# Neighbourhood attention: the second head's probabilities scaled by GpSimd, the bias loads issued between its steps

## What is computed

```python
s_loc = einsum(qr, kr) * scale + bias          # 8 rows x 32 columns of keys around the query
s_loc = where(mask, s_loc, -inf)
s_ctx = einsum(qr, kc) * scale                 # the 256 context keys
p = softmax(concatenate([s_loc, s_ctx], -1), -1)
o = einsum(p_loc, vr) + einsum(p_ctx, vc)
y_c = o * silu(cz)
```

## Time and profile before

| | |
|---|---|
| runs, median (lowest to highest) | 3112.86 us (3111.77 to 3113.13) |
| the profiled execution, its own time | 3115.25 us |
| its span, first to last instruction | 3113.5 us |
| TensorE busy | 2975.4 us, 96% of the span |
| DVE busy | 1497.5 us, 48% |
| ScalarE busy | 1155.9 us, 37% |
| GpSimd busy | 147.6 us, 5% |

### The profile page before, as it was taken

One profiled execution on the slowest core, in us unless ns is written; L12 is line 12 of the kernel. 1 busy time (PEld: TensorE's weight loads), 2 busy tenths in 40 slices (PEclk: granted clock), 3 DMA queues, 4 the chain that ended last, 5 costly groups with the idle time before them and its releaser, 6 DMA issues.

```text
span 3113.5 us, 38501 instructions
## 1 busy us (share of the span) xinstructions
PE 2975.4 (96%) x15486; PEld 2424.6 (78%) x15486; DVE 1497.5 (48%) x2136; ACT 1155.9 (37%) x1828; POOL 147.6 (5%) x206
## 2 busy tenths in 40 slices
PE   7999999999999998989999999999999899999998
PEld 5767888777788887867888878868877678888776
DVE  4645454645454657267252542263444735353454
ACT  4335233425352344136233331163221634251352
POOL 1000000010000000000000400100000000120100
PEclk9999999999999999999999999999999999999999
DMA  4232322331332221110211211211111022222322
GB/s 178 95 142 101 122 108 101 113 122 68 109 107 91 97 90 54 68 48 4 74 42 62 90 67 54 95 59 61 54 61 68 21 77 67 90 88 81 112 75 81
DMA packets 44460, 256.79 MB, mean 82 GB/s; under 512 B 6344, under 2 KB 6352, under 8 KB 20512
## 3 DMA queue, kind: packets, MB, share of 16 engines
q1 hardware_dynamic: 30528, 204.30, 18.5%
q0 software_dynamic: 13792, 50.51, 5.0%
HBM read 250.51 MB, written 4.28 MB: 82 GB/s over the span
## 4 chain that ended last, share of the span: by engine, by line
PE 84%; DVE 9%; ACT 3%; issue 1%; DMA 1%; POOL 1%; DVEq 0%; SPq 0%; ACTq 0%
PE PS L805 13%; PE PS L806 13%; PE PS L807 13%; PE PS L786 7%; PE PS L785 7%; PE PS L787 7%; PE PS L751 2%; PE PS L750 2%; PE PS L749 2%; DVE SMALL L2392 2%; PE PS L986 1%; DMA W<-in_w 1%; PE PS L698 1%; PE PS L594 1%; PE PS L596 1%
## 5 line engine op out<-in xcount | busy, mean ns | idle before, releaser
L805 PE MATMUL PS<-HHX,WHX 128*128 128x512 f32 (+1 forms) x1456 | 511.2, 351 | 9.9 <-DVE WLX L2242 7.0
L806 PE MATMUL PS<-HL,WHX 128*128 128x512 f32 (+1 forms) x1456 | 512.3, 352 | 0.0
L1559 ACT ACTIVATE WHX<-W 128x2048 fp32r<-128x2048 f32 (+1 forms) x102 | 174.6, 1712 | 578.9 <-DMA W<-in_w 391.3
L807 PE MATMUL PS<-HHX,WLX 128*128 128x512 f32 (+1 forms) x1024 | 357.6, 349 | 0.0
L2242 DVE TENSOR_TENSOR WLX<-W,WHX 128x2048 fp32r<-128x2048 f32 x60 | 137.5, 2292 | 383.4 <-ACT WHX L1559 383.4
L805 PEld LDWEIGHTS PS<-HHX,WHX 128*128 128x128 f32 x1456 | 278.8, 191 | 48.4 <-DVE WLX L2242 7.8
L806 PEld LDWEIGHTS PS<-HL,WHX 128*128 128x128 f32 x1456 | 277.5, 191 | 36.6
L786 PE MATMUL PS<-HL,WH 128*128 128x512 f32 x672 | 265.4, 395 | 0.0
L785 PE MATMUL PS<-HH,WH 128*128 128x512 f32 x672 | 263.3, 392 | 0.0
L2242 DVE TENSOR_TENSOR WL<-W,WH 128x2048 fp32r<-128x2048 f32 x68 | 155.9, 2292 | 221.7 <-ACT WH L1559 221.6
L787 PE MATMUL PS<-HH,WL 128*128 128x512 f32 x672 | 261.7, 389 | 0.0
(11 more groups left out here) (533 smaller groups left out, 5902.4 us busy)
## 6 DMA issues: line engine op xcount, KB each, us to landing
W<-in_w SPq DMA_DIRECT2D x172, 1024.0 KB, 4.7
XC<-in_wm POOLq DMA_DIRECT2D x12, 1024.0 KB, 5.1
H<-in_wm POOLq DMA_DIRECT2D x12, 1024.0 KB, 5.7
W<-in_wb SPq DMA_DIRECT2D x24, 512.0 KB, 3.2
W<-in_w SPq DMA_DIRECT2D x8, 768.0 KB, 4.1
ARENA<-mrow POOLq DMA_DIRECT2D x12, 256.0 KB, 4.1
ARENA<-wrow POOLq DMA_DIRECT2D x12, 256.0 KB, 4.6
PR<-in_nbias POOLq DMA_DIRECT2D x12, 256.0 KB, 2.9
```

The costliest lines, as they stand in the source:

```text
L805: pe.matmul(dst, wh[:, s, c], hi[:, k, t0:t1], start=k == 0, stop=False)
L806: pe.matmul(dst, wh[:, s, c], lo[:, k, t0:t1], start=False, stop=False)
L807: mm = pe.matmul(dst, wl[:, s, c], hi[:, k, t0:t1], start=False, stop=k == kb - 1)
L1559: act.activation(dst[:, s, 0:n], W[:, s, 0:n], ACT.Copy).then_inc(wh_ready[s], 1)
```

## The change

- DVE scales head 0 alone; GpSimd scales head 1, with `tensor_scalar` by the same reciprocal, and counts a new semaphore `na_far`. TensorE's transposes of head 1 wait for `na_far`.
- The reciprocal counts a new semaphore `na_rec` in place of DVE's own step counter; DVE waits for it as it did for its own, and GpSimd waits for it ahead of its scaling.
- GpSimd goes through the steps in order. It issues load `i` after the scaling of the last step that uses load `i - 2`, and no longer waits for `na_max`.
- Two semaphores are saved elsewhere: the eight loads of the LRU weights count `loaded_pool`, so that whoever waits for the start's loads waits for nine of GpSimd's, and `ml_w` becomes a second count of `ml_l`.

```diff
-        eng.wait_ge(loaded_pool, 16)
+        eng.wait_ge(loaded_pool, 16 * 9)
...
-        pe.wait_ge(sem("lru_w"), 16 * 8)
+        pe.wait_ge(loaded_pool, 16 * 9)
...
-                pe.wait_ge(sem("na_probs"), past("na_probs", ly) + 2 * e["s"] + hh + 1)
+                done = ("na_probs", "na_far")[hh]
+                pe.wait_ge(sem(done), past(done, ly) + e["s"] + 1)
...
-                    act.activation(WQ[0:8, :, :], WQ[0:8, :, :], ACT.Exp).then_inc(sem("ml_w"), 1)
+                    act.activation(WQ[0:8, :, :], WQ[0:8, :, :], ACT.Exp).then_inc(sem("ml_l"), 1)
...
-            own.link(dve.reciprocal(SMALL[:, 32 + p:32 + p + n], SMALL[:, 16 + p:16 + p + n]))
+            dve.reciprocal(SMALL[:, 32 + p:32 + p + n], SMALL[:, 16 + p:16 + p + n]).then_inc(sem("na_rec"), 1)
+            dve.wait_ge(sem("na_rec"), past("na_rec", ly) + e["s"] + 1)
             v = NE[:, e["s"] % 2, :, :].rearrange("p a b -> p (a b)")
-            for i in range(n):
+            for i in range(n // 2):
                 c = slice(i * w, (i + 1) * w)
                 ins = dve.tensor_scalar(v[:, c], v[:, c], SMALL[:, 32 + p + i:33 + p + i], None, ALU.mult)
-                if (i + 1) * w % T == 0:
-                    ins.then_inc(sem("na_probs"), 1)
+            ins.then_inc(sem("na_probs"), 1)
...
-                pool.wait_ge(sem("ml_w"), past("ml_w", st.layer) + 1)
+                pool.wait_ge(sem("ml_l"), past("ml_l", st.layer) + 2)
...
-                for i in range(2, 12):
-
-                    last = max(e["s"] for e in steps if e["load"] == i - 2 and not e["ctx"])
-                    pool.wait_ge(sem("na_max"), past("na_max", ly) + last + 1)
-                    bias(ly, i)
+                for e in steps:
+                    p = 4 * (e["s"] % 2)
+                    pool.wait_ge(sem("na_rec"), past("na_rec", ly) + e["s"] + 1)
+                    v = NE[:, e["s"] % 2, 1, :]
+                    k = 2 if e["ctx"] else 1
+                    for i in range(k):
+                        c = slice(i * T // k, (i + 1) * T // k)
+                        ins = pool.tensor_scalar(v[:, c], v[:, c], SMALL[:, 32 + p + k + i:33 + p + k + i], None, ALU.mult)
+                    ins.then_inc(sem("na_far"), 1)
+                    for i in range(2, 12):
+                        if max(x["s"] for x in steps if x["load"] == i - 2 and not x["ctx"]) == e["s"]:
+                            bias(ly, i)
```

More of the change, by code:

```diff
@@ L467, in build @@
         ml_zm=n_ml, ml_o=n_ml, ml_dens=n_mu, ml_divf=n_mu, ml_divb=n_mu, ml_rs=n_mu, ml_scaled=n_mu,
-        ml_turned=n_mu, ml_y=n_mu, ml_w=1, ml_stored=64, ml_rows=1, ml_l=1, ml_ac=1, ml_emc=1,
+        ml_turned=n_mu, ml_y=n_mu, ml_stored=64, ml_rows=1, ml_l=2, ml_ac=1, ml_emc=1,
         bz_silu=6, cv_done=4, gate_mm=2, gate_f=2, gate_cols=2, wg_hi=1, wg_lo=1, wg_loaded=16, bqk=8, cv_scaled=8, rope_loaded=32,
-        rope_done=8, na_probs=2 * n_na, na_max=n_na, na_values=n_na, v_stored=16 * 8, v_blocks=16 * 7,
+        rope_done=8, na_probs=n_na, na_rec=n_na, na_far=n_na, na_max=n_na, na_values=n_na, v_stored=16 * 8, v_blocks=16 * 7,
         **{f"ml_bm{k}": 16 * slot_uses[k] for k in range(4)}, **{f"ml_bw{k}": 16 * state_uses[k] for k in range(4)})
@@ L2878, in _ @@
                                         64 * half:64 * half + 64],
-                                   lru_w[g, half, :, 2 * q:2 * q + 2, :]).then_inc(sem("lru_w"), 16)
+                                   lru_w[g, half, :, 2 * q:2 * q + 2, :]).then_inc(loaded_pool, 16)
         pool.wait_ge(w_ready[1], 16)
```

## The result

The changed kernel takes 3147.73 us, median of 4 runs (3144.22 to 3152.13), against 3112.99 us for the kernel before, measured beside it: ratio 1.0106, 95% interval 1.0094 to 1.0118. It is slower, as forecast, but by 1.1% where 0.5% was forecast; it lies 7 us above the range. The profiled execution took 3149.49 us, 34.2 more than the one of before.

The account below looks back on a forecast made before the run. TensorE was taken to bound the kernel, with DVE close behind. Less DVE work (-2.6), head 1 late (+3.6) and late bias loads (+14.4) summed to +15.4 us: 3128.3 us against the runs' median, range 3119 to 3141.

Parts of the forecast that it names:

- The nine-count start wait: At the kernel's start, waiting for nine of GpSimd's loads instead of one was claimed to cost nothing.
- The scaling's price: GpSimd's scaling of head 1, 128x512, was taken as 0.8 us, between bounds of 0.63 and 1.27 us.
- The prediction is wrong if the scaling takes over 1.5 us: Failure sign stated beforehand for GpSimd's scaling of head 1, which was forecast at 0.8 us.
- The start: GpSimd's scaling was claimed to begin behind DVE's head 0, 0.7 us after the reciprocal's start (R).
- Head 1: TensorE's transposes: head 1 just in time in paced steps, 0.3 us late in 12 waiting steps, +2.1 and +1.5 us.
- relief: DVE loses a scaling; about three late steps a layer shed 0.44 us each, -2.6 us in all.
- The late loads: Layer 1: six bias loads behind GpSimd's scaling make DVE's maxima wait 2.4 us each, +14.4 us.
- The clock: Rival: TensorE's clock falls after three pairs of stalls, 1.5 us each, +4.5 us, 3133 us; chance 0.07.
- The sum: Whole kernel: relief -2.6, head 1 +3.6, late loads +14.4, together +15.4 us.

Follow-up runs that it names:

- e7: Kernel before, bias loads released by the reciprocal of their last user's step; DVE scales both heads, GpSimd only issues: 3125.26 us, ratio 1.0032.
- e8: Kernel before, bias loads released when TensorE's transposes of their last user's step end; DVE scales both heads, GpSimd only issues: 3140.76 us, ratio 1.0084.
- e3: Changed kernel, with GpSimd's scaling also waiting until DVE has scaled head 0: 3153.67 us, ratio 1.0121.
- e4: Changed kernel, with GpSimd's tensor_scalar replaced by a tensor_tensor whose second input is the broadcast reciprocal: 3147.07 us, ratio 1.0095.
- e2: Changed kernel, but DVE scales both heads and GpSimd runs a same-shape stand-in on a spare tile, loads behind it: 3144.34 us, ratio 1.0089.
- e1: Changed kernel, with bias loads 2 to 11 issued by SyncE on the old na_max release; GpSimd still scales head 1: 3127.45 us, ratio 1.0041.
- e5: Changed kernel, with identity transposes filling TensorE's gaps in layer 1, at its start and in six late steps: 3142.28 us, ratio 1.0088.
- e9: Kernel before, with 20 identity transposes while TensorE waits at the start of layer 1: 3115.53 us, ratio 1.0004.
- e6: Changed kernel, with GpSimd scaling only half of head 1, DVE the rest, and SyncE issuing the loads early: 3118.72 us, ratio 1.0010.

## Why the prediction was wrong in size and right in kind

**What held.** The direction; that the late bias loads cost most; that they are six, all in layer 1, and that layer 0 with its distance of three steps hardly feels them (DVE never waited for nbias there in after; e7 and e8: +0.9 and +1.4 us). Landing took 2.8 to 3.6 us, median 2.9, as in the earlier trace rows. The nine-count start wait, `ml_l` and `na_rec` weren't tried by themselves; in this pair of profiles they share at most the 0.6 us that the two stages leave of the 34.2.

**The scaling's price** (the step "I take 0.8 us", with 1.27 as upper bound) is the term that failed. It is 1.85 us, 1.56 of it its own (e3). Both bounding rows were of other operations: one that reads one tensor and one that reads two. Neither bounded a tensor_scalar with its scalar from SBUF. The same engine multiplied by the same scalar in 1.04 us when it was given as a broadcast second tensor (e4). "The prediction is wrong if the scaling takes over 1.5 us" was the right alarm, but the range had no room for it.

**The start** was taken at R+0.7, behind DVE. GpSimd began at R+0.26 and lost 0.29 us to DVE; counted to the end, 0.7 + 1.56 = R+2.26 against R+2.11, the two agree within 0.2 us. The Trainium skill, "SBUF — State Buffer", section "Who interferes with whom", says that the one that issues first keeps the shared ports for its whole instruction. In after DVE starts 0.05 us ahead of GpSimd and keeps its 0.49 us; there the trace agrees. In e4 one of the two waits for nearly all of the other's time, but not in that order: DVE, 0.04 us ahead, was the one that needed 1.37 us, until 0.29 us after GpSimd's end. e2 does not fit at all: beside a GpSimd instruction of 1.85 us DVE's second scaling was delayed by some 0.4 us, not until its end.

**Head 1** was put at R+1.5, and so at +3.6 us in 12 steps less 2.6 of relief. It came at R+2.16. TensorE waited 11.3 us for it in the two layers. e1 measures that term and the relief together: its two stages grew by 6.7 + 4.6 = 11.3 us, some 1 us of it by the clock, where +1.0 was expected. That this is also the sum of TensorE's waits is chance.

**The late loads** were put at 2.4 us each. DVE waited 3.5 (20.9 over 6). Two things add: issue at R+2.06 in place of R+1.5, and that DVE came to the bias at R+1.3 and not at R+2.03. The latter was read from a step that TensorE paces; behind a stall the scores lie ready, so DVE wants the bias earlier. The period is set by the load alone, 2.06 + 2.9 + 1.07 = R+6.0, as the timeline shows, where R+5.5 was forecast. The six late intervals were 38.3 us against 19.0 for the same steps before: +19.3 where 14.4 was forecast.

**The clock** was a rival of its own at 0.07: "TensorE's clock falls in the stalls", +4.5 us. It came on top of the mechanism, not in its place. The three intervals after gaps, with the same steps of before at 3.12, 3.70 and 3.70 us, make +7.6 us, 5.0 of which e5 gave back; its whole effect in layer 1 was 5.7. Of the 5.0 us, 1.2 lie in the step behind the gap ahead of the stage. That gap is in the kernel before too, which also ran at half clock behind it: its first two intervals took 6.47 us, 5.84 with e9's matmuls and 7.24 in after. So the late loads' own price in the clock is nearer to 4 us, close to the rival's 4.5. The prediction expected TensorE busy for 3.1 us of each 5.5 and at 2.4 GHz; ahead of the drop it was busy for 1.37 of 4 us. In layer 0 of after two more stretches ran at half clock, 2047.4 to 2054.2 and 2112.3 to 2119.1, and the two intervals there grew by 1.6 and 2.2 us. No run was made for them, but others hold the same steps at 2.4 GHz: 3.35 us in e1 where after took 4.51, and 5.09 in e5 where after took 5.91. Some 2 us of layer 0's 8.0 are thus clock, which the prediction did not have for that layer.

**The sum** as it stands: layer 1, +19.3 for the six late steps, +7.6 for the three behind gaps, -1.3 for all others, is +25.6. Layer 0, +8.0, of which e1 without late loads had 6.7. The forecast had +14.6 and +0.8 for them. From the other side it is 11.3 for the scaling (e1) and 22.3 for what stood behind it.

**Relief** (-2.6 us in the forecast) was not measured by itself. In e1 TensorE waited 4.3 us less for DVE than before, so it is somewhere within the net 11.3 us; e6 took no work off DVE and cannot show it. No version here beat the kernel before.

**In short**: two terms were too small. The scaling with the wait for head 1, less the relief, was +1.0 and came to 11.3 us; the late loads were +14.4 and came to 21.0 us, what e1 gave back in layer 1, with the slow clock behind them in it (0.8 of the 21.0 is the clock at the start of the stage). The forecast of the direction was no luck, since the wait that it named is the one that the trace shows.

## What to carry to other kernels

Before a transfer's issue is put behind a compute step, take the distance from the release to the first use, as the consumer would reach it after a stall, and subtract issue and landing: with two steps of distance an issue 0.5 us behind the reciprocal cost 8 us here and one 2 to 3 us behind it 24, with three steps 1.4 at most. A helper engine's instruction is priced by a record of that very operation; rows of neighbouring operations are no bound, and work taken off an engine that isn't the bound paid nothing here that could be told from noise, while each wait that it added was real. Where stalls are forecast in the engine that sets the pace, give the slow clock of the work behind them a term in the sum, with a range that starts at nothing: it was some 4 us here.

## What the runs showed of the hardware that was not expected

- GpSimd's tensor_scalar of 128x512 with the scalar from SBUF takes 1.56 us alone, and 0.92 us for 128x256 (e3): 2.5 ns an element. The tensor_tensor with the scalar broadcast took 1.04 us (e4), less than the 1.27 us of two whole tiles.
- Started within 0.05 us of each other, DVE's scaling and GpSimd's tensor_scalar cost GpSimd 0.29 us and DVE nothing; beside GpSimd's tensor_tensor, in most steps DVE lost 0.88 us and GpSimd nothing, in others GpSimd 0.29 and DVE nothing (e4). A second DVE scaling that begins while GpSimd's tensor_scalar runs is slowed too: two of 128x512 took 1.32 us in place of 0.96 (e2).
- Bias loads issued by SyncE landed in 2.5 to 2.6 us (e1), by GpSimd in 2.9.
- In after the clock stayed at 1.2 GHz for between 3 and 7 us at a time, four times in layer 1. The last idle piece of TensorE over 1 us ahead of each was 2.7, 1.9, 1.8 and 3.1 us long. A gap of 2.7 us ahead of layer 1 lowered it in before and not in e7.
